# The first feed-forward group of a streaming encoder layer, with its products ordered by chunks of tokens

## What is computed

```python
def rms_norm(x, g):
    xf = x.astype(jnp.float32)
    y = xf * lax.rsqrt(jnp.mean(xf * xf, axis=-1, keepdims=True) + RMS_EPS)
    return (y * g.astype(jnp.float32)).astype(x.dtype)
...
    h = rms_norm(x, lw['norm_g'][0]) * (1 + sc_a) + sh_a
    m, ckv_new, krope_new, S_new, shift_new = mixer(h, pos, ckv_past, krope_past, wkv0, shift0, lw)
    x = x + gt_a * rms_norm(m, lw['norm_g'][1])
    h = rms_norm(x, lw['norm_g'][2]) * (1 + sc_f) + sh_f
    f = (jax.nn.silu(h @ lw['w_gate']) * (h @ lw['w_up'])) @ lw['w_down']
    x = x + gt_f * rms_norm(f, lw['norm_g'][3])
```

## Time and profile before

| | |
|---|---|
| median of 3 runs | 2024.68 us |
| lowest and highest | 2020.99 and 2035.16 us |
| profiled execution | 2033.99 us, of which the span is 2031.9 us |
| TensorE busy in the span | 1888.2 us (93%) |
| VectorE, ScalarE, GpSimd busy | 959.9, 620.1, 339.1 us |
| mean granted TensorE clock | 0.973 of 2.4 GHz |

### The profile page before, as it was taken

The page is one execution under the profiler, slowest core; times in us unless marked ns, Lnnn a source line. Parts: engine busy times, 40 slices in busy tenths (PEclk is TensorE's granted clock), DMA queues, the critical chain, the costliest instruction groups (busy, mean ns, idle before and its releaser), DMA issues.

```text
span 2031.9 us, 42591 instructions
## 1 busy us (share of the span) xinstructions
PE 1888.2 (93%) x17546; PEld 1598.0 (79%) x17546; DVE 959.9 (47%) x1534; ACT 620.1 (31%) x1254; POOL 339.1 (17%) x408
## 2 busy tenths in 40 slices
PE   5999999898999999998999949999999999999996
PEld 3988898477577577676644639999999999999995
DVE  4696765545645545655323242332332342342347
ACT  4644423244344344434322222121021111011114
POOL 0033320235533434434400010000000000000000
PEclk9999999899999998998999969999999999999998
DMA  8357773011111011102221011111121021011032
GB/s 328 113 167 207 182 194 133 24 45 42 33 39 49 26 39 35 40 25 83 82 96 49 30 70 34 60 52 33 41 63 41 24 63 43 21 63 52 11 119 88
DMA packets 125608, 149.20 MB, mean 73 GB/s; under 512 B 83088, under 2 KB 98064, under 8 KB 124976
## 3 DMA queue, kind: packets, MB, share of 16 engines
q1 hardware_dynamic: 125424, 146.47, 23.0%
HBM read 115.95 MB, written 30.50 MB: 72 GB/s over the span
## 4 chain that ended last, share of the span: by engine, by line
PE 84%; DVE 7%; issue 3%; ACT 2%; DMA 1%; SPq 0%; POOL 0%; DVEq 0%; ACTq 0%; POOLq 0%
PE ps L436 35%; PE ps L2198 11%; PE ps L2173 6%; PE ps L2041 4%; PE ps L1932 3%; PE ps L1940 3%; PE ps L474 3%; PE ps L2070 3%; PE ps L2055 2%; PE ps L2125 2%; PE ps L2091 2%; PE ps L2109 2%; PE ps L1943 2%; PE ps L1865 2%; DVE scr L1414 1%
## 5 line engine op out<-in xcount | busy, mean ns | idle before, releaser
L436 PE MATMUL ps<-fhi,whi 128*128 128x364 f32 (+1 forms) x1056 | 351.2, 333 | 25.1 <-DVE flo L1362 15.9
L436 PE MATMUL ps<-flo,whi 128*128 128x364 f32 (+1 forms) x1056 | 349.2, 331 | 0.0
L436 PE MATMUL ps<-fhi,wlo 128*128 128x364 f32 (+1 forms) x1056 | 348.1, 330 | 0.0
L436 PEld LDWEIGHTS ps<-fhi,whi 128*128 128x128 f32 x1056 | 200.5, 190 | 27.5 <-DVE flo L1362 16.8
L428 DVE TENSOR_TENSOR wlo<-wraw,whi 128x1024 fp32r<-128x1024 f32 x66 | 82.2, 1246 | 287.6 <-ACT whi L424 284.7
L436 PEld LDWEIGHTS ps<-fhi,wlo 128*128 128x128 f32 x1056 | 201.1, 190 | 0.0
L436 PEld LDWEIGHTS ps<-flo,whi 128*128 128x128 f32 x1056 | 200.5, 190 | 0.0
L436 PE MATMUL ps<-hhi,whi 128*128 128x364 f32 (+1 forms) x480 | 167.6, 349 | 11.2 <-DVE hlo L1362 10.9
L1750 DVE TENSOR_TENSOR acc<-acc,ps 128x364 f32<-128x364 f32 (+1 forms) x240 | 126.6, 532 | 102.4 <-PE ps L2198 102.4
L825 POOL TENSOR_TENSOR nlev<-gm,con 64x256 f32<-64x256 f32 x204 | 154.3, 756 | 121.0 <-DVE gm L1517 107.0
L2198 PE MATMUL ps<-ahi,dhi 128*128 128x364 f32 (+1 forms) x480 | 158.9, 331 | 2.5 <-DVE acc L1750 2.4
(11 more groups left out here) (231 smaller groups left out, 3246.6 us busy)
## 6 DMA issues: line engine op xcount, KB each, us to landing
wraw<-in_w_tiles SPq DMA_DIRECT2D x64, 512.0 KB, 4.2
late<-in_ada_t SPq DMA_DIRECT2D x32, 512.0 KB, 3.7
ci<-scan SPq DMA_DIRECT2D x17, 768.0 KB, 4.3
draw<-in_w_down SPq DMA_DIRECT2D x20, 512.0 KB, 3.6
slab<-in_ada_w SPq DMA_DIRECT2D x4, 2048.0 KB, 17.8
x<-in_x_t SPq DMA_DIRECT2D x4, 1456.0 KB, 10.1
bg<-bg SPq DMA_DIRECT2D x17, 256.0 KB, 2.7
x<-x_mid SPq DMA_DIRECT2D x1, 4352.0 KB, 12.9
```

The costliest lines, as they stand in the source:

```text
L436: mm = nc.tensor.matmul(ps[:, 3 * u + c, 0:n], w[u][:, k, :], x[:, k, :], start=(k == 0 and i == 0), stop=(k == KD - 1 and i == 2))
```

## The change

The first group is made in another order, by chunks. Both halves are run for t = 0 and t = 1, and then both for t = 2. As the slots of the weight buffers hold only one half's tiles, each of the four tiles is loaded and split twice: the pair numbers PRE_M and PRE_M + 1 are the two halves for the first two chunks, FF_M and FF_M + 1 the same tiles again for the last chunk (FF_TILE shifts the index so that they are the same). TensorE's norm sum "m" of t = 2 stands behind the first product, the sum "n2" behind the fourth; four products of half 1 follow it, and then the four products of t = 2. Each of `out_ready`'s counts for a pair must still come to three, so some products count two or three steps. ScalarE's and VectorE's orders are written out to match: the first Silus, products and splits stand between the steps of the norm chain of t = 2. The buffers `ahi` and `alo` become two pieces each; those of slot 0 lie where `yt` (the mixer's output of one head group) was, so they can be written before x2 is done with, and `acc` moves behind them. The wait of ScalarE for the three stores of x2 goes. In the diff, the rest of which renames arguments, "..." stands for lines left out.

```diff
-        acc, ahi, alo, draw, dhi0, dhi1, dlo0, dlo1, sil0, sil1, sil2, end = place(
-            R2, ("acc", [P, KD, T]), ("ahi", [P, 4, T], F32R), ("alo", [P, 4, T], F32R), ("draw", [P, D]),
+        ahi0, alo0, acc, ahi2, alo2, draw, dhi0, dhi1, dlo0, dlo1, sil0, sil1, sil2, end = place(
+            R2, ("ahi0", [P, 2, T], F32R), ("alo0", [P, 2, T], F32R), ("acc", [P, KD, T]), ("ahi2", [P, 2, T], F32R), ("alo2", [P, 2, T], F32R),
+            ("draw", [P, D]),
...
+        ahi, alo = {0: ahi0, 2: ahi2}, {0: alo0, 2: alo2}
@@ -384,8 +386,10 @@
-        FF_M = OUT_M
+        PRE_M = OUT_M
+        FF_M = PRE_M + 2
         END_M = FF_M + 2 * GROUPS
+        FF_TILE, PRE_TILE = KD - 4, KD
@@ -715,13 +719,17 @@
             for u in range(2):
-                load_weight(sp, FF_M, u, after=KD)
+                load_weight(sp, PRE_M, u, after=PRE_TILE)
             store_x2(0)
             sp.wait_ge(hi_ready, 8)
             sp.wait_ge(lo_ready, 4)
             load_x2(2)
+            for u in range(2):
+                load_weight(sp, PRE_M + 1, u, after=PRE_TILE)
             for t in range(1, 3):
                 store_x2(t)
+            for u in range(2):
+                load_weight(sp, FF_M, u, after=FF_TILE)
             sp.wait_ge(lo_ready, 6)
-            load_weight(sp, FF_M + 1, 0, after=KD)
-            load_weight(sp, FF_M + 1, 1, after=KD)
+            load_weight(sp, FF_M + 1, 0, after=FF_TILE)
+            load_weight(sp, FF_M + 1, 1, after=FF_TILE)
...
@@ -1275,11 +1283,10 @@
                         for u in range(2):
-                            split_hi(act, FF_M, u)
-                for part in ("m", "n2"):
-                    out_part(t, part)
-            for part in OUT_PARTS.values():
-                out_part(2, part)
+                            split_hi(act, PRE_M, u)
+                if t < 2:
+                    for part in ("m", "n2"):
+                        out_part(t, part)
...
@@ -1288,28 +1295,58 @@
-            def gate(g, slot, j, first=False, last=False):
+            def gate(g, slot, j, last=False):
 
                 m = 2 * g + FF_M + j
                 q = 6 * g + 3 * j
                 for c, (a, n) in enumerate(CH):
-                    act.wait_ge(out_ready[0], 3 * m + (max(c, 1) if first and j == 0 else c) + 1)
-                    if not (first and j == 0):
-                        act.wait_ge(act_lo, q + c - 2)
+                    act.wait_ge(out_ready[0], 3 * m + c + 1)
+                    act.wait_ge(act_lo, q + c - 2)
                     nc.scalar.activation(sil[c][:, 0:n], ps[:, c, 0:n], ACT.Silu).then_inc(sil_ready, 1)
                 if not last:
                     split_hi(act, m + 1, 0)
-                if not first:
-                    act.wait_ge(down_ready, 24 * (g - 1) + 1)
+                act.wait_ge(down_ready, 24 * (g - 1) + 1)
                 for c, (a, n) in enumerate(CH):
                     act.wait_ge(prod_ready, q + c + 1)
-                    nc.scalar.copy(ahi[:, slot + j, a:a + n], sil[c][:, 0:n]).then_inc(act_hi, 1)
+                    nc.scalar.copy(ahi[slot][:, j, a:a + n], sil[c][:, 0:n]).then_inc(act_hi, 1)
                 if not last:
 
-            act.wait_ge(x2_out, 48)
-            gate(0, 0, 0, first=True)
-            gate(0, 0, 1, first=True)
+            def silu(m, c, order, ready, free):
+
+                a, n = CH[c]
+                act.wait_ge(out_ready[0], 3 * m + ready)
+                at_least(act, act_lo, free)
+                nc.scalar.activation(sil[c][:, 0:n], ps[:, c, 0:n], ACT.Silu).then_inc(sil_ready, 1)
+
+            def high(j, c, order):
+
+                a, n = CH[c]
+                act.wait_ge(prod_ready, order)
+                nc.scalar.copy(ahi[0][:, j, a:a + n], sil[c][:, 0:n]).then_inc(act_hi, 1)
+
+            c0, c1, c2 = OUT_ORDER
+            out_part(2, "m")
+            silu(PRE_M, c0, 1, 1, 0)
+            silu(PRE_M, c1, 2, 3, 0)
+            split_hi(act, PRE_M + 1, 0)
+            out_part(2, "n2")
+            split_hi(act, PRE_M + 1, 1)
+            high(0, c0, 1)
+            high(0, c1, 2)
+            out_part(2, "n2 root")
+            out_part(2, "split")
+            silu(PRE_M + 1, c0, 3, 1, 1)
+            silu(PRE_M + 1, c1, 4, 3, 2)
+            split_hi(act, FF_M, 0)
+            high(1, c0, 3)
+            high(1, c1, 4)
+            split_hi(act, FF_M, 1)
+            for j in range(2):
+                silu(FF_M + j, c2, 5 + j, 3, 4 + j if j else 0)
+                split_hi(act, FF_M + j + 1, 0)
+                high(j, c2, 5 + j)
+                split_hi(act, FF_M + j + 1, 1)
@@ -1681,7 +1718,7 @@
             for u in range(2):
-                split_lo(dve, FF_M, u)
+                split_lo(dve, PRE_M, u)
@@ -1713,17 +1750,50 @@
+            def gated(m, j, c, order, ready):
+
+                a, n = CH[c]
+                dve.wait_ge(sil_ready, order)
+                dve.wait_ge(out_ready[1], 3 * m + ready)
+                nc.vector.tensor_tensor(sil[c][:, 0:n], sil[c][:, 0:n], ps[:, 3 + c, 0:n], ALU.mult).then_inc(prod_ready, 1)
+
+            def low(j, c, order):
+
+                a, n = CH[c]
+                dve.wait_ge(act_hi, order)
+                nc.vector.tensor_tensor(alo[0][:, j, a:a + n], sil[c][:, 0:n], ahi[0][:, j, a:a + n].bitcast(F32), ALU.subtract).then_inc(act_lo, 1)
+
+            c0, c1, c2 = OUT_ORDER
             dve.wait_ge(gains_done, 4)
-            for t in range(3):
+            for t in range(2):
                 residual(t)
                 feed(t)
+            residual(2)
+            gated(PRE_M, 0, c0, 1, 1)
+            gated(PRE_M, 0, c1, 2, 3)
+            split_lo(dve, PRE_M + 1, 0)
+            low(0, c0, 1)
+            low(0, c1, 2)
+            split_lo(dve, PRE_M + 1, 1)
+            feed(2)
+            gated(PRE_M + 1, 1, c0, 3, 1)
+            gated(PRE_M + 1, 1, c1, 4, 3)
+            split_lo(dve, FF_M, 0)
+            low(1, c0, 3)
+            low(1, c1, 4)
+            split_lo(dve, FF_M, 1)
+            for j in range(2):
+                gated(FF_M + j, j, c2, 5 + j, 3)
+                split_lo(dve, FF_M + j + 1, 0)
+                low(j, c2, 5 + j)
+                split_lo(dve, FF_M + j + 1, 1)
...
@@ -1762,8 +1832,6 @@
 
             dve.wait_ge(acc_zero, 1)
-            product(0, 0, 0, first=True)
-            product(0, 0, 1)
@@ -2195,7 +2263,7 @@
...
-                            mm = nc.tensor.matmul(ps[:, 6 + x % 2, 0:n], w[u][:, P * k:P * k + P], y[:, slot + u, a:a + n],
+                            mm = nc.tensor.matmul(ps[:, 6 + x % 2, 0:n], w[u][:, P * k:P * k + P], y[slot][:, u, a:a + n],
...
@@ -2213,16 +2281,27 @@
             pe.wait_ge(m_ev, 3 * KD)
-            for t, c in enumerate(OUT_ORDER):
-                if t == 2:
-                    for name in ("m", "n2"):
-                        norm_sum(pe, name, sq2, c)
+            def first_product(m, u, t, steps):
+
+                c = OUT_ORDER[t]
                 pe.wait_ge(lo_ready, 3 + t + 1)
+                pe.wait_ge(w_lo, 2 * m + u + 1)
+                chunk_product(u, c, True).then_inc(out_ready[u], steps)
+
+            first_product(PRE_M, 0, 0, 1)
+            norm_sum(pe, "m", sq2, OUT_ORDER[2])
+            first_product(PRE_M, 1, 0, 1)
+            for u in range(2):
+                first_product(PRE_M, u, 1, 2)
+            norm_sum(pe, "n2", sq2, OUT_ORDER[2])
+            for t in range(2):
                 for u in range(2):
-                    pe.wait_ge(w_lo, 2 * FF_M + u + 1)
-                    chunk_product(u, c, True).then_inc(out_ready[u], 1)
-            for u in range(2):
-                ff_project(0, 1, u)
+                    pe.wait_ge((sil_ready, prod_ready)[u], t + 1)
+                    first_product(PRE_M + 1, u, t, 1 + t)
+            for j in range(2):
+                for u in range(2):
+                    at_least(pe, (sil_ready, prod_ready)[u], 5 * j)
+                    first_product(FF_M + j, u, 2, 3)
             group(1, 2)
             down(0, 0, first=True)
```

More of the change, by code:

```diff
@@ L737, in _ @@
                     for u in range(2):
-                        load_weight(sp, 2 * g + FF_M + j, u, after=KD)
+                        load_weight(sp, 2 * g + FF_M + j, u, after=FF_TILE)
                 load_down(g - 1, 1)
@@ L742, in _ @@
                 for u in range(2):
-                    load_weight(sp, END_M - 2 + j, u, after=KD)
+                    load_weight(sp, END_M - 2 + j, u, after=FF_TILE)
             load_down(GROUPS - 2, 1)
@@ L1724, in down_lo, with product @@
                 nc.vector.tensor_tensor(dlo[u][:, :], draw[:, :], dhi[u][:, :].bitcast(F32), ALU.subtract).then_inc(d_lo, 1)
-            def product(g, slot, j, last=False, adding=None, first=False):
+            def product(g, slot, j, last=False, adding=None):
                 m = 2 * g + FF_M + j
@@ L1733, in product @@
                     dve.wait_ge(sil_ready, q + c + 1)
```

(6 more changed lines are left out.)

## The result

The changed kernel took 2002.5 us in the median of four runs (1999.1 to 2004.8), beside 2026.4 us for the kernel before; the ratio is 0.9877, with a 95% interval of 0.9852 to 0.9901. The profiled execution has a span of 2001.9 us, 30.0 less than the one before.

The account below looks back on a forecast made before the run. TensorE was taken as the bound, idling 13.0 and 15.9 us in the norm chain. 1239.47 less 1214.7 gave 24.8 us, less 0.8 for the clock 24.0: median 2024.7 to 2000.7 us, range 1996 to 2011.

Parts of the forecast that it names:

- the stretch: TensorE from the feed-forward's first product to the second group's first product: 92.35 us before, forecast to lose 24.8 us.
- Part 1: TensorE, last chunk's sum "m" moved up: after a new 2.3 us gap it ends at 1158.6 instead of 1168.56.
- Part 2: Three products under the chain to sum "n2": TensorE idles 0.6 us; ScalarE has 1.5 us to spare, VectorE 0.9.
- Part 3: Four half 1 products under the rest of the norm chain: TensorE's second wait, before 15.9 us, hidden by 0.7 us.
- Part 4: VectorE's splits behind gated products: TensorE waits about 1.8 us at three places, before FF_M, FF_M + 1 and second group.
- Part 5: Four tiles loaded again, four more splits each on ScalarE and VectorE: costs nothing beyond the three waits for VectorE's splits.
- Part 6: Two more ScalarE table switches in the norm chain, 1.28 us per load: nothing; 0.3 us by the Trainium skill's figure.
- The clock: Low clock after TensorE's new waits: half of 1.7 us for the 2.3 us gap, 0 for the three others; 0.8 us.
- the late chain: Rival: ScalarE or VectorE slips one product, 4.1 us, in each cover of the norm chain; gain 16.5, 2008.2 us; chance 0.11.
- the sum that isn't earlier: Rival: last chunk's sum "m" still ends at 1168.6; gain only 14.8, kernel 2009.9 us; chance 0.05.
- the late reloads: Rival: second weight loads of FF_M + 1 and second group land late; at 15.7 us, 8 us slower, 2032.7; chance 0.04.
- The rival of the clock: Rival: clock falls in two to four of TensorE's new gaps, 1.7 us each; gain 18.0 to 21.4 us; chance 0.18.

## Why the prediction was right

It gave 2000.7 us; 2002.5 was measured. The 1.8 us between them are those by which the median of the kernel before rose with a fourth run, from 2024.7 to 2026.4 us: the gain in the medians is 24.0 us, as forecast, with an interval of 20 to 30 us. The gain of the stretch was forecast as 24.8 us without the clock and came as 24.8. The mechanism is the one forecast, but the agreement to a tenth is partly luck, since errors of opposite sign met: the seven products behind the two sums were taken at 4.14 us each and took 4.0, 1.0 us less in all, while the waits of parts 2 and 4 came to 0.7 us more and the five other products to 0.4 more. By its parts, counted from the first product:

- **Part 1.** The first sum starts after 6.5 us and ends after 11.6; 6.4 and 11.5 were forecast. The run with the sum alone shows what it is worth: 13.0 us, of which 9.9 are the chain's earlier start, 2.5 the second sum at full clock and 0.7 less low clock behind the second wait (0.79 over the last chunk's products, against 0.75).
- **Part 2.** A wait of 0.98 us where 0.6 was forecast, as the three products took 12.0 us and not 12.4. The two steps that could have been late were not: ScalarE waited 1.99 us for x2 (1.5 forecast) and VectorE 1.08 us for the root (0.9 forecast).
- **Part 3.** The low part of the last chunk was there after 45.4 us (45.5 forecast), and TensorE's four products hid it, by 0.25 us where 0.7 was forecast. Half the cover taken away came back one for one.
- **Part 4.** Three waits of 1.8 to 1.9 us, 5.7 in all (5.4 forecast), each released by VectorE's split. Moving the splits took 4.6 us off, so they were what TensorE waited for.
- **Part 5.** The second loads cost nothing: their slack was reckoned as 3.8 us and measured as 4.1. Loads took longer to land than before (the median from 1040 us on is 4.5 us, against 3.7), and that fitted in.
- **Part 6.** The new switches lay where they were put, and none was waited for: the load before the root "n2" ended 0.94 us before the root could start, and behind the third the split was done at 1189.8, 1.0 us before VectorE came to it. Two more before the root made it late.
- **The clock.** Here the step was only partly right. The new wait of 2.2 us before a sum had no price in any of the seven profiles that hold it (the sum took 5.08 us each time), where I had set half of 1.7. The waits of 1.9 us, at which I had set nothing, do have one at times: of 12 pairs of products right behind such a wait, three took 9.7 us instead of 8.1. One of the three stood behind a pair that had been slow already. In the two profiles of the changed kernel none did, so the 0.8 us set for the clock were not paid there; a fall behind one of the three waits would have cost twice that. The prediction also rested on one wait of 3.3 us without a fall; the same trace has waits of 2.8 and 2.5 us of the same kind, at 1456.8 and 1606.0, with a fall behind each, which it didn't weigh.

Of the rivals, the late chain, the sum that isn't earlier and the late reloads did not happen, and each has its run: ScalarE made 3.0 us late makes TensorE wait 2.1 us longer, putting the sum back costs 14.3 us, and a reload must be 4.1 us late before it costs anything. The rival of the sum priced it at 10.0 us less gain (24.8 less 14.8) and left out the low clock behind the bare wait, which is 4.3 of the 14.3. The rival of the clock didn't happen in either profile of the changed kernel; its other executions have no profile. Of the 2.6 us on either side of the stretch, those behind it are in the main one fall of the clock more in the kernel before; those ahead of it lie within the spread of that part (below). Neither is shown to come from the change.

## What to carry over

When the bound engine idles through a long dependent chain on other engines, look first at what starts the chain: here the sum stood in TensorE's queue behind three products that it didn't need, and moving it alone gave half the gain. Then cover the rest with work whose inputs exist, even if operands must be loaded twice, and write the next step's weight split ahead of any operation that waits for the bound engine. Where the rest of the program varies more than the edit, compare two kernels by the stretch that was changed too, and not by whole times alone.

## What was not expected of the hardware

**The rest of the program varies by the clock.** The first product of the feed-forward network, ahead of which TensorE does the same work in all kernels, stood between 1133.4 and 1147.1 us in eleven profiles. The two ends, by stretches of 100 us (length, busy time of TensorE, its weight loads, VectorE, ScalarE and GpSimd, granted clock, DMA share, GB/s); first the kernel before:

```profile
700.00:800.00 100.00, 94.52 (x1555) 70.90 (x1553) 52.65 (x108) 40.84 (x98) 43.76 (x60) 0.95 0.10 32
900.00:1000.00 100.00, 90.97 (x1699) 70.64 (x1698) 52.96 (x119) 41.95 (x115) 48.53 (x68) 0.95 0.19 56
```

and the run with the sum moved back:

```profile
700.00:800.00 100.00, 92.40 (x1654) 70.32 (x1652) 52.88 (x109) 42.60 (x104) 41.47 (x58) 1.00 0.10 33
900.00:1000.00 100.00, 90.88 (x1697) 68.20 (x1694) 50.12 (x116) 41.03 (x113) 48.87 (x69) 1.00 0.26 77
```

In the same code the clock fell to its lower level in some executions and not in others, while TensorE's busy share was alike. An estimate of the most that this can cost, from the rows: 0.05 of the clock over 100 us is 5 us of full clock, so the two stretches shown make 10 us, and the two that begin at 600 and 800 us (0.98 against 1.00 each) 4 more, beside a difference of 13.7 us between the two starts. The whole times point the same way: in 38 executions of the kernel before, from 2016.7 to 2033.8 us, time and mean granted clock have a correlation of -0.81. That the clock is the cause of the spread was not tested.

**The length of a wait does not tell its price.** A wait of 3.3 us left the clock at 1.00, one of 2.2 us in front of a sum after the projection was followed by a fall in 9 of 11 profiles, one of 2.2 us in front of the same kind of sum after a product in none of seven, one of 1.9 us in three of 12, and one of 1.8 us before the second group in none of seven. The three waits at the loop's start show both ends at one length. Behind 2.82 us in the kernel before, and behind 2.76 us in the changed one:

```profile
1460.00:1464.00 4.00, 4.00 (x17) 4.00 (x17) 0.00 (x0) 0.00 (x0) 0.00 (x0) 0.62 0.00 0
1581.00:1585.00 4.00, 4.00 (x24) 4.00 (x25) 0.00 (x0) 0.00 (x0) 0.00 (x0) 1.00 0.02 4
```

Over the eleven profiles there are 33 such waits, of 2.5 to 3.3 us; the clock fell behind 16 of them (0.57 to 0.68 over the next 4 us), and the waits with a fall (2.5 to 3.1 us) and without (2.5 to 3.3 us) overlap in length. What decides it these runs don't show.
